# An expert layer in split precision: dot products moved beside the one-hot rows, fifteen of sixteen groups made ahead

## The reference

```python
s = einsum('thpd,hpnd->thpn', q, keys)         # 8 heads, 2 x 128 keys
top_s, top_i = top_k(s, 16)                    # then the best 16 of 256 pairs
idx, g = ...                                   # per token: 128 slots, an expert (of 16384) and a gate each
act = gelu(einsum('td,thkd->thk', x, u_tab[idx]))
out = einsum('thk,thkd->td', g * act, v_tab[idx])
```

## Time and profile before

| | us |
|---|---|
| median of 3 runs | 3963.34 (3960.61 to 3970.87) |
| the profiled execution's own time | 3959.03 |
| its span | 3957.2 |
| PE busy | 3571.5 (90%), 17547 matmuls |
| DVE busy | 2270.8 (57%) |
| POOL busy | 1708.3 (43%), of which 1581.8 in 649 low parts |
| ACT busy | 1385.4 (35%) |
| DMA | 794.62 MB, 201 GB/s in the mean |

### The profile page before, as it was taken

The page is one execution under the profiler, slowest core; times in us unless marked ns, Lnnn a source line. Parts: engine busy times, 40 slices in busy tenths (PEclk is TensorE's granted clock), DMA queues, the critical chain, the costliest instruction groups (busy, mean ns, idle before and its releaser), DMA issues. The chain is left out here.

```text
span 3957.2 us, 50913 instructions
## 1 busy us (share of the span) xinstructions
PE 3571.5 (90%) x17547; PEld 3021.3 (76%) x17547; DVE 2270.8 (57%) x4241; ACT 1385.4 (35%) x2049; POOL 1708.3 (43%) x781
## 2 busy tenths in 40 slices
PE   8999898899899999968989999988888999998788
PEld 5777676677777787736776667787888999988788
DVE  4562346422333553176755654599999566667787
ACT  4332233322443322223232443233366434433332
POOL 5765332233333443322333113344323667656555
PEclk9999998999999999979999999998999999999889
DMA  7997853455564464313242126844356889878875
GB/s 250 378 388 252 276 160 119 135 169 164 173 203 151 144 192 132 93 52 107 91 137 91 61 69 225 318 138 132 124 187 234 305 311 332 308 290 323 312 292 218
DMA packets 427309, 794.62 MB, mean 201 GB/s; under 512 B 28392, under 2 KB 293544, under 8 KB 407114
## 3 DMA queue, kind: packets, MB, share of 16 engines
q1 hardware_dynamic: 291104, 475.39, 36.0%
q10 hardware_dynamic: 117610, 182.91, 13.8%
q0 software_dynamic: 18432, 134.23, 8.9%
HBM read 673.40 MB, written 186.12 MB: 217 GB/s over the span
## 5 line engine op out<-in xcount | busy, mean ns | idle before, releaser
L534 POOL TENSOR_TENSOR weights_lo<-weights_raw,weights_hi 128x1024 fp32r<-128x1024 f32 x649 | 1581.8, 2444 | 2211.2 <-ACT weights_hi L1216 2205.7
L607 PE MATMUL bank<-operand_hi,weights_hi 128*128 128x512 f32 (+1 forms) x2856 | 1095.2, 383 | 64.3 <-DVE operand_lo L1895 24.0
L609 PE MATMUL bank<-operand_hi,weights_lo 128*128 128x512 f32 (+1 forms) x2856 | 1065.2, 373 | 0.0
L608 PE MATMUL bank<-operand_lo,weights_hi 128*128 128x512 f32 (+1 forms) x2856 | 1065.0, 373 | 0.0
L1216 ACT ACTIVATE weights_hi<-weights_raw 128x1024 fp32r<-128x1024 f32 x649 | 680.3, 1053 | 984.4 <-PE bank L609 660.2
L607 PEld LDWEIGHTS bank<-operand_hi,weights_hi 128*128 128x128 f32 x2856 | 542.2, 190 | 157.4 <-DVE operand_lo L1895 30.2
L608 PEld LDWEIGHTS bank<-operand_lo,weights_hi 128*128 128x128 f32 x2856 | 542.9, 190 | 74.9 <-issue 6.1
L609 PEld LDWEIGHTS bank<-operand_hi,weights_lo 128*128 128x128 f32 x2856 | 541.5, 190 | 75.0
L607 PE MATMUL bank<-expert_hi,weights_hi 128*128 128x384 f32 x1024 | 358.8, 350 | 87.7 <-POOL weights_lo L534 84.6
L608 PE MATMUL bank<-expert_lo,weights_hi 128*128 128x384 f32 x1024 | 353.6, 345 | 0.0
L609 PE MATMUL bank<-expert_hi,weights_lo 128*128 128x384 f32 x1024 | 352.7, 344 | 0.0
(11 more groups left out here) (397 smaller groups left out, 4872.8 us busy)
## 6 DMA issues: line engine op xcount, KB each, us to landing
weights_raw<-in_w_ffn_gu SPq DMA_DIRECT2D x132, 512.0 KB, 5.7
weights_raw<-in_w_peer SPq DMA_DIRECT2D x112, 512.0 KB, 6.4
expert_table<-expert_turned ACTq DMA_DIRECT2D x288, 128.0 KB, 4.8
expert_table<-in_w_peer_out SPq DMA_DIRECT2D x72, 512.0 KB, 5.5
weights_raw<-in_w_peer_ahead SPq DMA_DIRECT2D x72, 512.0 KB, 3.8
weights_raw<-in_w_peer_out SPq DMA_DIRECT2D x72, 512.0 KB, 7.1
expert_table<-in_w_peer SPq DMA_DIRECT2D x56, 512.0 KB, 5.4
expert_rows<-in_w_peer ACTq DMA_DIRECT2D x54, 512.0 KB, 6.9
```

The costliest lines, as they stand in the source:

```text
L534: pool.tensor_tensor(LO[:, slot, :], RAW[:, slot, :], HI[:, slot, :].bitcast(F32), ALU.subtract).then_inc(sem("lo_ready"), 1)
L607: pe.matmul(out, wh, hi(k), start=(k == 0), stop=False)
L608: pe.matmul(out, wh, lo(k), start=False, stop=False)
L609: ins = pe.matmul(out, wl, hi(k), start=False, stop=(k == kc - 1))
```

## The change

**Counts.** `AHEAD` 9 to 15 and `SHARED` 7 to 1: 15 groups "in" are made beside routing (15 units a tile, 60) and beside the one-hot rows (60 units over 96 quarters, 5 steps a quarter), one group is left to the shared stage. All 16 groups "out" follow.

**Slots.** The table is cut in two, key rows and value rows, so that a slot is two gathers of 128 x 1024 numbers, in a ring of five. The first 96 dots (`EARLY`) stand beside the one-hot rows, one after each quarter; 32 dots and all 128 sums stand in the first 120 units "out" (`late_operations`, `late_at`), 4 in 3 units. The dots of many slots are summed, opened by gelu and weighed at once (`sum_dots`, `open_slots`, `weigh_slots`) instead of one by one.

**Pieces.** One low part and one gated product per unit "out" instead of two in the first four. PE waits for them step by step in a group's first unit.

**Loads.** Gates and gelus of a group are loaded a group ahead, from ACT's queue, behind the high part of the fourth and eighth piece; there are two buffers for the gates. The gates lie in DRAM by group, so that the store of 16 tokens has runs of 512 bytes and the load of a group one run per partition. SP's queue holds only weights, and the stages' stores.

**Also** DVE may be three quarters ahead of PE (16 one-hot buffers, before 8), PE's one-hot loop and group loop are written out, `peer_sum` starts with a copy instead of zeros.

The core of the diff:

```diff
-AHEAD = 9
-BY_TILE = 12
-BY_TURN = 4
+AHEAD = 15
+BY_TILE = 15
+BY_TURN = 10
-DEEP = 4
+DEEP = 5
+EARLY = 96
...
-def steps_of_group(g):
...
+QUARTERS = 16 * GATE_TURNS
+PER_QUARTER = BY_TURN * UNIT // 16
+HOT_UNITS = BY_TURN * GATE_TURNS
+
+def late_operations():
+    rest = SLOTS - EARLY
+    mixed = [op for i in range(rest) for op in (("dot", EARLY + i), ("add", 2 * i), ("add", 2 * i + 1))]
+    return mixed + [("add", s) for s in range(2 * rest, SLOTS)]
+
+def late_at(u):
+    count, units = len(late_operations()), UNIT * (EXP_GROUPS - 1)
+    return range(count * u // units, count * (u + 1) // units) if u < units else range(0)
...
 # POOL
-            for s in range(DEEP, SLOTS):
-                after.setdefault(dense + place_of[s - DEEP + 1] + 4, []).append(s)
+            unit_of = [PER_QUARTER * q // UNIT - HOT_UNITS for q in range(EARLY)]
+            unit_of += [8 * SHARED + u for u in range(UNIT * EXP_GROUPS) for _ in late_at(u)]
+            for k in range(len(sources)):
+                after.setdefault(hot0 if k < DEEP else hot0 + HOT_UNITS + unit_of[k - DEEP] + 4, []).append(k)
...
 # ACT
+            for q in range(QUARTERS):
+                stage(q)
+                hot_units(PER_QUARTER * q // UNIT)
+            hot_units(HOT_UNITS)
...
+            def ahead_high(o, u):
...
+                expert_high(buffers[:, u, :], WF[:, u % 2, :], 8 * SHARED + 8 * o + u)
+                if u % 4 == 3 and o + 1 < AHEAD:
+                    load_gelus(o + 1, u // 4)
+                if u == 7 and SHARED + o + 2 < EXP_GROUPS:
+                    load_group_gates(SHARED + o + 2)
...
+            for v in range(EXP_GROUPS):
+                for c in range(8):
+                    units(1)
+                    ahead_high(v + (c + 1) // 8, (c + 1) % 8)
...
 # DVE
+            for q in range(QUARTERS):
+                wait(dve, sem("gates_done"), q - 3)
+                for u in range(4):
+                    t = P + 4 * q + u
+                    ins = hot(slice(t, t + 1), 4 * (q % 4) + u)
+                ins.then_inc(sem("hot_ready"), 1)
+                dot(q)
...
+            for v in range(EXP_GROUPS - 1):
                 for c in range(8):
+                    dve.wait_ge(sem("pe_steps"), s1 + UNIT * (c + 1) + 8 * UNIT * v)
+                    ahead_low(v, c)
+                    ahead_gated(v + (c + 1) // 8, (c + 1) % 8)
+                    add(v, c)
+                    late(8 * v + c)
```

More of the change, by code:

```diff
@@ L399, in program @@
         STB = BANK[4]
+        tokens_in, sums_of = (BANK[4], BANK[7]), (BANK[5], BANK[6])
         def vec(name, c=0):
@@ L522, in _ @@
+            issued = RING
+            for k in range(QUARTERS // 4):
+                for v in range(issued, min(HOT_UNITS + RING, BY_TURN * (k + 1) // 4 + 5)):
+                    hot_unit(v)
+                    issued = v + 1
+                store_stage(k)
+            for v in range(issued, HOT_UNITS + RING):
+                hot_unit(v)
+            part("peer", RING)
+            part("peer_out")
             for c in range(DC):
@@ L543, in _, with gather @@
                     low(RING * i + u, u)
-            def gather(s):
-                if s == 0:
+            sources = [("dot", s) for s in range(EARLY)] + late_operations()
+            def gather(k):
+                which, s = sources[k]
+                if k == 0:
                     pool.wait_ge(sem("values_copied"), 16 * 8 * EXP_GROUPS)
-                    for which in TABLE:
-                        into = len(ROWS[which][1])
+                    for part in TABLE:
+                        into = len(ROWS[part][1])
@@ L571, in _ @@
             for n in range(RING * turns, TOTAL):
                 low(n, n % RING)
-                for s in after.pop(n, []):
-                    gather(s)
+                for k in after.pop(n, []):
+                    gather(k)
             assert not after
@@ L2497, in _, with gathered, dot @@
             dve.wait_ge(sem("turned"), turns1 + TT - 1)
+            rows = {"used": 0, "added": 0}
+            def gathered():
+                k = rows["used"]
+                rows["used"] += 1
+                dve.wait_ge(sem(f"gathered{k % DEEP}"), 16 * (k // DEEP) + 16)
+                return RB[:, k % DEEP, :]
+            def dot(s):
+                row = gathered()
+                if s == 0:
+                    dve.wait_ge(sem("tokens_ready"), 4)
+                for h in range(2):
+                    half = row[:, TOK * h:TOK * h + TOK]
+                    ins = dve.tensor_tensor_reduce(half, half, tokens_in[h][:], 1.0, 0.0, ALU.mult, ALU.add,
+                                                   DOT[:, s, h:h + 1])
+                ins.then_inc(sem("rows_used"), 1)
@@ L2604, in step, with late @@
-            def step(steps, u):
-                if u in steps:
-                    dot()
-                    if slots["dotted"] > 1:
-                        add_values()
+                ins.then_inc(sem("rows_used"), 1)
+            operations = late_operations()
+            last_dot = max(k for k, op in enumerate(operations) if op[0] == "dot")
+            def late(u):
+                for k in late_at(u):
+                    which, s = operations[k]
+                    if which == "dot":
+                        dot(s)
+                    else:
+                        add_values(s)
+                    if k == last_dot:
+                        sum_dots(EARLY, SLOTS)
```

396 lines of the change are left out of this document (147 added, 249 removed).

## The result

The changed kernel takes 4035.99 us in the median of 4 runs (4031.21 to 4044.40); the kernel before took 3965.07 in the median of its 4 runs by then (3960.61 to 3970.87). The ratio is 1.0181, with a 95% interval from 1.0168 to 1.0195: slower by 71 us. The profiled execution took 4032.64 us, its span 4030.8, at a mean granted clock of 0.949.

The account below looks back on a forecast made before the run. After the change, the gathers' chain was to bound the one-hot stage and the ring the value stage. Terms 277 + 498 + 38 + 615 + 37 = 1465 us against 1387, +78, gave 4040 us; range 3940 to 4120.

Parts of the forecast that it names:

- the gathers' chain: One-hot stage: a gather stands behind POOL's low part, whose split follows ACT's staging; two waits per 8 quarters, stage 498 us.
- the ring: Value stage: gated product, high part, split, POOL's low part, DVE's held low part, gated product again; 4.96 us a unit.
- Routing: Routing stage with 60 units: PE needs 69.2 us for each of four tiles, DVE no later; 277 us.
- One-hot stage: 60 units over 96 quarters, set by late gathers: twelve periods of 41.1 us plus 5; 498 us, bounds 452 and 546.
- G: Time from a gather's issue to landing in the one-hot stage: 3.9 to 7.8 us, taken as 5.8.
- T = 5.9 + G: One-hot stage: time after a quarter's rows until the dependent dot, through PE, ACT, POOL and the gather; 11.7 us.
- First group: First 8 dense units after the one-hot stage: 33 us plus 5 for gates stored and loaded first; 38 us.
- Value stage: 15 groups at 41.0 us: eight units of 4.96 us plus three load issues on ACT at 0.45; 615 us.
- Rival 1: Value stage: the ring doesn't hold, DMA decides at 34.9 us a group; 92 us less, 3948 us; chance 0.12.
- Rival 2: One-hot stage: the gathers' chain doesn't bind; stage 390 + 5, 103 us less, 3937 us; chance 0.08.
- Rival 3: Slower than forecast: gathers among one-hot rows land late, or ACT is held in load issues; about 4110 us; chance 0.15.
- Rival 4: Value stage: loads a group ahead bring nothing, the ring leaving PE 7 us waiting per group; part of the forecast, 4040.

Follow-up runs that it names:

- the run with the gathers later: Changed kernel with each early gather one weight unit later in POOL's order: 4464.7 us, one-hot stage 954.3 us.
- without loads: Changed kernel with the value stage's loads of gates and gelus left out after the first ahead group: 4039.8 us, 39.0 a group.
- the early gathers: Changed kernel with the one-hot stage's early gathers two weight units earlier in POOL's order: 3912.5 us, stage 407.6 us.
- the splits ahead: Changed kernel with gathers two units earlier, plus ACT's value-stage splits one weight unit ahead of the high parts: 3834.5 us, 33.4 a group.
- the narrow run: Changed kernel with the value stage's slot operations cut to 8 of 512 columns: 3957.2 us, 33.4 a group.
- the tie: Gathers two units earlier and splits one unit ahead, plus POOL's value-stage low parts also waiting for DVE's gated product: 3836.0 us, against 3834.5 without.

## Why the prediction was right

4040 was said and 4036 measured, but that it came so close is luck: two terms missed by 35 and 39 us in opposite directions and covered each other. What was right without luck are the two mechanisms, the gathers' chain and the ring, and with them that the change is slower.

- **Routing**, 277 said, 270.6 measured. PE pays for the added units, and DVE's lists, the cause of 28.6 us of waiting in the earlier trace rows, are no longer late (2.4 us). The sum has a slip: it takes a third of the 28.6 us off each of four tiles, where a quarter gives 59.1 us a tile and 286 in all. That would be 16 us too much, and it takes PE's time from a stage with a granted clock of 0.91, where it was 1.00 after. The prediction also says that 36 units move; it is 48, 12 to this stage and 36 to the one-hot stage, and the terms use the right counts.
- **One-hot stage**, 498 said, 533 measured. The mechanism was right: gathers placed earlier and later show it from both sides. G, the gather's time to land, was right (5.6 us in the median among the rows, 5.8 over all). The mis-sized term is T = 5.9 + G: 11.7 said, 13.6 in the turn shown, and 12.3 from the run with the gathers later. It lacks the dense steps that stand on PE ahead of the one-hot matmuls: the rows are ready at 3066.48, and PE comes to them at 3068.54, 2.1 us later. Most of that is, in this turn, the lower clock, which the sum put at nothing: the one-hot matmuls of the quarter before and the dense steps behind them took 2.07 and 3.30 us, and 1.05 and 2.69 one quarter on, so at full clock PE would have come about 0.5 us after the rows (an estimate from these four numbers). The count was off too: DVE waits 52 times, 4.3 in eight quarters and not 2, and 13.1 us in all of them (157.6 / 12), so each wait is 3.0 us in the mean and not the 5 to 9 said. The period is 525.7 / 12 = 43.8 us, which the formula put at 41.1: 2.7 twelve times are about 33 of the 35 us.
- **First group**, 38 said, 37 measured.
- **Value stage**, 615 said, 576 measured, 41.0 us a group against 38.6. The ring was right, with its condition. Of the 2.4 us, 0.7 are its period (4.87, not 4.96), 1.3 the load issues, which don't lengthen it, and 0.4 the units in which they open it (39.0 without loads). That term had the wrong sign. The sign of PE waiting 6 to 8 us a group didn't come: it waits 3.0 (45.2 / 15). Most of the rest of the 5.3 us between 38.6 and PE's 33.3 is PE at a lower clock, 0.96 in the stage: it is busy for 35.2 us a group.
- **End**, 37 said, 38.8 measured.
- **Rival 1 and 2.** Both would have been the right reading one place away in the order. Rival 2 was priced at 103 us, and the early gathers give 124 by the medians; rival 1 at 92, and the splits ahead give 78. Both together were put at 3845, and 3834.5 was measured. The 34.9 us that DMA was said to need for a group was too much: 33.4 were reached, at 377 to 380 GB/s. The condition given for rival 1, DVE at the low part under 1.7 us after the product, held in the narrow run; with the splits ahead the ring opened by POOL's phase, which the prediction didn't name.
- **Rival 3** did not come: the gathers among the rows landed as early as the others (5.6 us in the median against 6.2 in the value stage). **Rival 4** was said to hold, that the loads a group ahead bring nothing. The waits of the earlier trace rows did go, from 72.4 to 2.1 us, and the ring took that gain; which part of the change took them away wasn't parted.

The moves of the change are thus sound, 3.2% faster than before once two places in the order are mended, and these two places made it slower: gathers two weight units too far back, and splits one unit too far back.

What stays open: how much of the 42 to 45 us from the last row to the first gated product could be hidden, how much of the one-hot stage's 533 us the lower clock alone cost, and whether rows read from PSUM would escape POOL's hold; the last wasn't tried.

## What to carry to other kernels

When a transfer is placed by counting behind another engine's work, write down for each place which event releases it, back through all engines, and compare that with when it is needed: here one unit was worth 16, 102 and 429 us of the one-hot stage, growing from place to place. Where two engines hold each other up, try to release both from the same event, in the order in which they should run, so that the second works while the first does something that isn't held. The sign here was a period of 4.83 us, longer than any engine's own work, with DVE shown as 99% busy: part of that was waiting. And where an edit has two parts, run each without the other before believing the reason: the tie to which I gave the gain had no share in it.

## What the runs showed of the hardware

- Held time counts as busy. DVE is busy for 571.5 of 576 us in the value stage of the changed kernel, and for 404.7 of 490 with the splits ahead, where a group of the same work takes 33.4 us instead of 38.6. The low parts' median is 2.41 us in the one and 0.56 in the other.
- The hold goes both ways: POOL's low part takes 2.76 us instead of 2.40 where DVE's gated product is in ahead of it (3567.83 and 3567.87 in the rows above). The one-hot rows are held too, with one tensor in SBUF as input: 2.41 us instead of 0.34. The Trainium skill, "SBUF — State Buffer", section "SBUF: two separate sides", calls it an exclusive lock; the holds in both directions agree, and so does that the sums and dots, with one input in PSUM, keep their 0.67 to 0.76 us each in the whole value stage, beside POOL or not.
- After PE had waited 8.24 us for DVE, its eight one-hot matmuls took 2.07 us, and 1.05 a quarter later:

```profile
3063.51 2.07 PE L1102 MATMUL bank<-one_hot_j,one_hot_i 128*128 128x128 f32 x8 [8.24 <-DVE one_hot_j L2502]
```

  The granted clock around them was 0.50. With the gathers one unit later it is 0.71 in the one-hot stage and 0.908 over the run; with no gap in PE's work it is 1.00 over 480 us (narrow slot operations, value stage).
- A gather of 0.5 MB lands 5.8 us after its issue in the median, 4.1 at best and 15.7 at worst; 91 of them beside the rows left the stage at 407.6 us, against 409.6 without them.
